# A two-block kernel on one core: first input projection in three fp32r products, first inverse level by transposes, GpSimd's powers ahead of the bias masks

## The chip, the cores and the metric

The kernel runs on one core of a Trainium2 chip. The core has a matrix engine (TensorE, PE in the rows, its weight loads PEld), a vector engine (VectorE, DVE), a scalar engine (ScalarE, ACT), a general engine (GpSimd, POOL) and a queue engine that mostly starts transfers (SyncE, SP). Each runs its own instructions strictly in order and waits on semaphores for the others. The metric is the device time of one launch in microseconds, the median of some runs. One further execution is recorded by the profiler.

## The reference, cut to what matters

Two transformer blocks follow each other on 256 tokens of width 1024. What the change touches is in the first block, and one wait in the second:

```python
h = rmsnorm(x, attn_norm[l])
proj = jnp.einsum('bsd,de->bse', h, w_in[l])          # 1024 -> 3592 columns, fp32
mq, mk, mv, gqkv, gz, ga, gb = jnp.split(proj, offsets, axis=-1)
y_a = moba_attention(...)                             # causal attention on mq, mk, mv
gqkv = jax.nn.silu(causal_depthwise_conv(gqkv, conv_w[l]))
...                                                   # q and k l2-normed, decays from ga, beta from gb
sol = lax.linalg.triangular_solve(eye + A, rhs, left_side=True, lower=True, unit_diagonal=True)
...
x = x + jnp.einsum('bse,ed->bsd', mix, w_out[l])      # then a mixture of experts, then block 2
```

The second block begins with a norm, an input projection, and a norm of the query and key heads (each needs an inverse square root), and its second attention adds a bias with a mask to the scores.

## The kernel before

**Layout and staging.** Everything is fp32. Tokens lie in two blocks of 128. Weights come from memory as units of 1 MB (`unit512`, list `pre`) into a ring of eight slots (`NS = 8`). SP issues unit n+8 when TensorE has used unit n (`freed`). Work is handed over through PSUM banks: three that VectorE empties (`v_bank`, `v_take`), three that ScalarE empties (`a_bank`, `a_take`), each handed out in strict rotation. A bank is asked for only when the third before it has been emptied.

**First projection.** `hT` is the normed input, turned. `cols_T` (L508) computes two pairs of 128 output columns from two units, 256 tokens wide, with the weights as the stationary operand; `rows_nat` (L518) computes 512 output columns with the tokens stationary. A product in fp32 is two instructions in the trace. The order on TensorE is: the three groups of convolution inputs, the 8 gate columns, sums of squares of q and k (L574), the attention's v rows, its q columns, decay rows (L582, L587), its k columns, and z: block 0 ahead of the Gram products (L599 to L614), block 1 behind them.

**Beside it.** ScalarE empties the convolution inputs (`conv_inputs`, L1274), applies silu (L1279) and squares (L1283), then the square roots (L1300), the softplus parts (L1304 to L1307, each with a load of its function table), the attention inputs (L1287), the exponentials of the decays (L1320 to L1323) and z (L1328). VectorE runs three convolutions of four chunks each (`conv`, L1584 and L1586), `qk_norm1` twice (a reciprocal L1616 and a product L1617), and the decay matrices (L1661).

**Inverse.** `X` and `Y` begin as the identity (GpSimd, L2155). At each of seven levels GpSimd masks `BT` (L2162), TensorE multiplies it by `X` (`level_w`, L628), VectorE makes `Wm` of it (L1682), and TensorE multiplies `Y` and `Wm` (L639, L644). Between them stand one head of attention (L655, L662 to L664, L675) and one tile of modulation products (L536, L546).

**The mixture of experts** then streams its weights, and the second block follows. There VectorE's `qk_norm` runs six times: squares and sums, a request to GpSimd for the power -1/2 (`rsqrt` and `power`, L2139), then the products. GpSimd's program has the two bias masks (L2171), which wait for rows that come through a DMA from `rpb_pad`, ahead of these powers. TensorE turns the heads (L929), VectorE copies them (L1969), and the scores begin (L975).

**The split form** is used in the last stage of the program only (`split_product`, L434 to L436; `hidden`, L1077 and L1078): ScalarE rounds a unit to fp32r (the upper part, L1485), VectorE subtracts (the lower part, L2069), and three products upper-upper, lower-upper and upper-lower stand for one in fp32.

## Time and profile before

| | us |
|---|---|
| median of 3 runs | 919.78 |
| lowest and highest | 917.84, 921.96 |
| profiled execution, device time | 921.78 |
| its span, first to last instruction | 920.0 |
| TensorE busy | 838.2 (91%) |
| VectorE busy | 379.5 (41%) |
| ScalarE busy | 258.4 (28%) |
| GpSimd busy | 50.8 (6%) |

The profile's page shows shares of the span. A share is an average over stages that have different limits, so each stage is read in the timeline and in tables of short stretches. The device time of the profiled execution is 1.78 us more than its span, and 2.0 us more than the median.

### The profile page before, as it was taken

The page shows a single profiled execution, that of the slowest core. Times are in us where ns is not written, and L with a number is a line of the kernel's source. Part 1 is how long each engine was busy: PE and PEld are TensorE (multiplying, and loading weights), DVE is VectorE, ACT ScalarE, POOL GpSimd, SP SyncE. Part 2 cuts the span into 40 slices and gives each one's busy share as a digit, 9 for nine tenths or more (in the row PEclk, how much of TensorE's full clock was granted, in tenths as well). Part 3 has the DMA queues.
Part 4 walks back from the last instruction along what each step waited for, and adds up shares of the span by engine and source line. Part 5 has one row for each costly group of instructions (what it writes and reads, how often), then busy time and mean ns, then how long its engine had stood idle before and what let it go on. Part 6 is the DMA issues. An engine that isn't in the chain of part 4 may idle for free.

```text
span 920.0 us, 12562 instructions
## 1 busy us (share of the span) xinstructions
PE 838.2 (91%) x5119; PEld 566.7 (62%) x5119; DVE 379.5 (41%) x710; ACT 258.4 (28%) x416; POOL 50.8 (6%) x35
## 2 busy tenths in 40 slices
PE   8999999989998877677767799979999999999998
PEld 6867767856565432343234254467884788888886
DVE  1557144445260111011101325762424775665765
ACT  2252124421112221122112211034552343443431
POOL 1000042101000000000000004210000000000000
PEclk9999999989999997998899899999999999999999
DMA  9953445557496999999999993420000734654501
GB/s 328 310 193 107 168 183 185 206 205 274 143 385 243 386 408 409 409 409 409 409 408 409 406 317 100 181 92 1 1 1 1 274 137 139 234 176 159 207 1 46
DMA packets 117850, 208.40 MB, mean 227 GB/s; under 512 B 7561, under 2 KB 34474, under 8 KB 117682
## 3 DMA queue, kind: packets, MB, share of 16 engines
q1 hardware_dynamic: 114930, 203.52, 59.9%
q10 hardware_dynamic: 2816, 4.27, 1.6%
q8 instruction: 29, 0.48, 0.2%
q14 instruction: 11, 0.09, 0.0%
q0 software_dynamic: 64, 0.05, 0.0%
HBM read 206.74 MB, written 1.08 MB: 226 GB/s over the span
## 4 chain that ended last, share of the span: by engine, by line
PE 71%; DMA 13%; DVE 7%; issue 3%; POOL 2%; ACT 2%; SPq 2%; DVEq 0%; PEldq 0%; ACTq 0%; POOLq 0%
DMA arena<-in_w_down_dram 10%; PE psa L508 8%; PE psv L1077 5%; PE psa L1077 4%; PE psv L863 4%; PE psa L975 3%; PE psa L847 3%; PE psx L1000 3%; PE psx L536 3%; DMA arena<-rpb_pad 3%; PE psa L798 2%; PE psa L744 2%; PE psv L1078 2%; PE psa L1078 2%; PE psv L518 2%
## 5 line engine op out<-in xcount | busy, mean ns | idle before, releaser
L2069 DVE TENSOR_TENSOR unit_parts<-ring,unit_parts 128x2048 fp32r<-128x2048 f32 x33 | 75.6, 2290 | 59.2 <-ACT unit_parts L1485 59.2
L1485 ACT ACTIVATE unit_parts<-ring 128x2048 fp32r<-128x2048 f32 x33 | 63.2, 1914 | 74.9 <-PE psa L1078 43.8
L905 PE MATMUL psa<-ring,arena 128*128 128x512 f32 (+1 forms) x192 | 76.1, 558 | 2.0 <-DVE arena L1550 1.2
L863 PE MATMUL psv<-ring,arena 128*32 128x256 f32 x1024 | 59.4, 381 | 17.6 <-DMA ring<-in_w_up_dram 13.3
L508 PE MATMUL psa<-arena,ring 128*128 128x256 f32 x320 | 69.9, 380 | 1.0 <-ACT arena L1253 1.0
L1077 PE MATMUL psv<-column_parts,unit_parts 128*128 128x512 f32 (+1 forms) x192 | 67.0, 397 | 2.5 <-DVE arena L2096 1.4
L508 PEld LDWEIGHTS psa<-arena,ring 128*128 128x128 f32 x320 | 60.7, 190 | 10.2 <-DVE arena L1548 1.2
L1077 PE MATMUL psa<-column_parts,unit_parts 128*128 128x512 f32 (+1 forms) x192 | 65.4, 389 | 0.0
L905 PEld LDWEIGHTS psa<-ring,arena 128*128 128x128 f32 x192 | 36.4, 190 | 41.1 <-issue 37.3
L863 PEld LDWEIGHTS psv<-ring,arena 128*32 128x32 f32 x1024 | 32.2, 110 | 42.8 <-DMA ring<-in_w_up_dram 19.1
L1078 PE MATMUL psv<-column_parts,unit_parts 128*128 128x256 f32 (+1 forms) x192 | 52.8, 275 | 0.0
L1078 PE MATMUL psa<-column_parts,unit_parts 128*128 128x256 f32 (+1 forms) x192 | 52.1, 271 | 0.0
L1877 DVE TENSOR_TENSOR arena<-arena,psv 128x256 f32<-128x256 f32 x8 | 3.4, 421 | 116.0 <-ACT arena L1408 116.0
L2139 POOL TENSOR_TENSOR small<-small,consts 128x2 f32<-128x2 f32 (+4 forms) x15 | 21.8, 1454 | 511.5 <-DVE small L1897 274.3
L847 PE MATMUL psa<-arena 128*128 128x128 f32 x256 | 32.3, 287 | 15.5 <-DVE arena L1875 15.5
L847 PEld LDWEIGHTS psa<-arena 128*128 128x128 f32 x256 | 30.8, 201 | 22.1 <-issue 22.1
L1077 PEld LDWEIGHTS psv<-column_parts,unit_parts 128*128 128x128 f32 x192 | 37.1, 193 | 10.3 <-DVE unit_parts L2069 2.8
L1886 DVE TENSOR_TENSOR residual<-residual,psx 128x512 f32<-128x512 f32 x16 | 11.0, 688 | 76.8 <-PE psx L890 76.8
L1077 PEld LDWEIGHTS psa<-column_parts,unit_parts 128*128 128x128 f32 x192 | 36.2, 189 | 7.5
L1078 PEld LDWEIGHTS psv<-column_parts,unit_parts 128*128 128x128 f32 x192 | 37.4, 195 | 0.6 <-issue 0.2
L1078 PEld LDWEIGHTS psa<-column_parts,unit_parts 128*128 128x128 f32 x192 | 36.5, 190 | 0.0
L880 PE MATMUL psx<-arena 128*32 128x512 f32 x128 | 25.6, 896 | 9.6 <-DMA arena<-in_w_down_dram 9.6
(369 smaller groups left out, 1383.4 us busy)
## 6 DMA issues: line engine op xcount, KB each, us to landing
ring<-in_w_gate_dram SPq DMA_DIRECT2D x43, 1024.0 KB, 9.2
ring<-in_w_up_dram SPq DMA_DIRECT2D x43, 1024.0 KB, 5.2
arena<-in_w_down_dram SPq DMA_DIRECT2D x32, 1024.0 KB
ring<-in_w_in_dram SPq DMA_DIRECT2D x28, 1024.0 KB, 9.7
ring<-in_w_mod_dram SPq DMA_DIRECT2D x24, 1024.0 KB, 7.0
ring<-in_w_down_dram SPq DMA_DIRECT2D x11, 1024.0 KB, 7.3
ring<-in_w_out_dram SPq DMA_DIRECT2D x8, 1024.0 KB, 6.0
arena<-rpb_pad ACTq DMA_DIRECT2D x4, 512.0 KB, 16.4
```

Source lines behind the costliest of these rows:

```text
L508: mm = pe.matmul(bank[:, cc * T:(cc + 1) * T], w, hT[:, k, :], start=(k == 0), stop=(k == KD - 1))
L536: mm = pe.matmul(bank[32 * j:32 * j + 32, :], csil[:, k, :], units[r][:, j, :], start=(r == 0), stop=(r == 1))
L847: mm = pe.matmul(mXT[half][:, kk * P:(kk + 1) * P], h2[:, b, k * P:(k + 1) * P], Pd[:, b, :, :].rearrange("p e s -> p (e s)"), start=(b == ...
L863: mm = pe.matmul(mG[32 * e:32 * e + 32, f0:f0 + FF], XT[:, 2 * pair + kk, 32 * e:32 * e + 32], w[:, e, kk * FF:(kk + 1) * FF], start=(pair ...
L880: mm = pe.matmul(mY[half][32 * e:32 * e + 32, :], hidT[:, fc * P + 32 * e:fc * P + 32 * e + 32], w[:, e, :], start=(fc == 0), stop=(fc == 1))
L905: mm = pe.matmul(bank[:, 0:ncols], lhs[:, k, b * P:(b + 1) * P], units[k // per][:, k % per, :], start=(k == 0), stop=(k == KD - 1))
L975: mm = pe.matmul(o_, l_, r_, start=first, stop=last)
L1000: mm = pe.matmul(bank[:, h * HD:(h + 1) * HD], PT2[:, n % 4, m * P:(m + 1) * P], vs[m], start=(m == 0), stop=(m == 3))
L1077: pe.matmul(both_parts(bank, t_0, t_1), hi, col_parts[:, :, k, t_0:t_1], start=(k == 0), stop=False)
L1078: mm = pe.matmul(bank[:, t_0:t_1], lo, col_parts[:, 0, k, t_0:t_1], start=False, stop=(k == KD - 1))
L1485: act.activation(unit_parts[q % 3][:, 0, :], slot_of(NPRE + u_), ACT.Copy).then_inc(upper_done, 1)
L2069: vec.tensor_tensor(lo, slot_of(NPRE + at["mlp"] + 3 * n + kind), hi, ALU.subtract).then_inc(lower_done, 1)
```

## The change

1. **Split projection.** After the first four 128-column groups and the gate columns, which stay in fp32, twelve units (`FIRST_SPLIT` = 3 onward) are used as an upper and a lower part. ScalarE writes the upper part of unit s into one of three buffers (`first_upper_part`), VectorE writes the lower part over the ring slot (`first_lower_part`). The buffers lie over `hn`, `hT` and `mixT`, so upper part s waits until TensorE has used unit s-3 (`freed`). `hT` is split as well, into `row_hi` and `row_lo`; `row_lo` lies over the residual, so x is loaded again later. Eight of the twelve units are now 256 columns wide, with rows of 1 KB in memory instead of 2 KB.
2. **Order.** z is computed whole ahead of the Gram products, and takes both of its banks at the start; the first modulation tile stands behind them. The gate columns and the softplus come earlier on both ScalarE and VectorE.
3. **Level 0 of the inverse** needs no product: `X` and `Y` are not set to the identity any more, the masked `BT` is turned, VectorE writes its `Wm` straight into `X`, and `Y` is the transpose of that.
4. **GpSimd** runs the six `qk_norm` powers ahead of the two bias masks, and TensorE waits for a mask only when the first tile that uses it comes.

```diff
+        FIRST_SPLIT = len(pre)
+        for c0 in (2048, 2304, 2560, 2816):
+            unit512(pre, w_in, c0, 256)
+        unit512(pre, w_in, 1024)
+        for c0 in (0, 256, 512, 768):
+            unit512(pre, w_in, c0, 256)
+        unit512(pre, w_in, 3072)
...
+            def split_cols():
+                hi, lo = split_unit()
+                bank = a_bank()
+                for cc in range(2):
+                    for k in range(KD):
+                        mm = split_product(bank[:, cc * T:(cc + 1) * T], [w[:, k, cc * P:(cc + 1) * P] for w in (hi, lo)],
+                                           [r[:, k, :] for r in (row_hi, row_lo)], k == 0, k == KD - 1)
+                mm.then_inc(a_ready, 1)
+                freed.append((a_ready, na))
...
+            def split_rows(take, ready):
+                banks = [take(), take()]
+                for part in range(2):
+                    hi, lo = split_unit()
...
             def level_w(n):
                 pe.wait_ge(level_masked, n + 1)
-                if n == 0:
-                    pe.wait_ge(inverse_started, 2)
-                else:
+                if n > 0:
                     pe.wait_ge(a_free, na)
...
+                        if n == 0:
+                            mm = pe.transpose(bank[:, h * P:(h + 1) * P], masked, ident)
...
+            def first_upper_part(s):
+                u_ = FIRST_SPLIT + s
+                act.wait_ge(unit_landed[u_ % NS], 16 * (u_ // NS + 1))
+                if s >= 2:
+                    act.wait_ge(*freed[u_ - 3])
+                if s == 2:
+                    act.wait_ge(row_split, 1)
+                act.activation(first_upper[s % 3][:], slot_of(u_), ACT.Copy).then_inc(first_upper_done, 1)
...
+            def first_lower_part(s):
+                dve.wait_ge(first_upper_done, s + 1)
+                u_ = FIRST_SPLIT + s
+                vec.tensor_tensor(ring_parts[:, u_ % NS, :], slot_of(u_), first_upper[s % 3][:],
+                                  ALU.subtract).then_inc(first_lower_done, 1)
...
+            for nh in (2, 2, 8, 8, 8, 8):
+                power(rsn[:, 0:2 * nh])
             pool.wait_ge(s_bias_rows, 64)
```

**ScalarE's order in the first stage.** Before, from the second emptied bank of convolution inputs to the square roots (L1274 convolution inputs, L1279 silu, L1283 squares, L1300 square roots):

```order
L1274 ACTIVATE arena<-psa 128x2x256 [waits a_ready,pad_done]
L1274 ACTIVATE arena<-psa 128x2x256 [waits a_ready] x3
L1279 ACTIVATE arena<-arena 128x1024 [waits conv_done]
L1283 ACTIVATE arena<-arena 128x1024 [waits silu_done]
L1274 ACTIVATE arena<-psa 128x2x256 [waits a_ready]
```

After, the same stretch begins with upper parts 0 and 1 (L1348) and has the convolution inputs (L1356), silu (L1361) and squares (L1365) between them:

```order
L1348 ACTIVATE first_upper<-ring 128x2048 [waits unit_landed3]
L1348 ACTIVATE first_upper<-ring 128x2048 [waits unit_landed4]
L1356 ACTIVATE arena<-psa 128x2x256 [waits a_ready,pad_done]
L1356 ACTIVATE arena<-psa 128x2x256 [waits a_ready]
L1377 ACT_TABLE_LOAD [waits v_free,csil_ready]
L1377 ACTIVATE arena<-vec_cols 128x8 [waits s_const]
L1378 ACTIVATE arena<-vec_cols 128x8
L1348 ACTIVATE first_upper<-ring 128x2048 [waits row_split,v_ready,unit_landed5]
L1361 ACTIVATE arena<-arena 128x1024 [waits conv_done]
L1365 ACTIVATE arena<-arena 128x1024 [waits silu_done]
```

The first two convolution inputs now stand behind the landing of unit 4, and upper part 3 behind the silu of the first convolution.

**ScalarE at the decays** (L1320 and L1418 exponential of the sums, L1323 and L1421 of the decay matrices, L1287 and L1369 attention inputs). Before:

```order
L1287 ACTIVATE arena<-psa 128x512 [waits a_ready] x2
L1320 ACT_TABLE_LOAD
L1320 ACTIVATE small<-small 128x8 [waits log_decay_done]
L1322 ACTIVATE small<-small 128x4 [waits decay_arg_done]
L1323 ACTIVATE arena<-arena 128x1024
L1287 ACTIVATE arena<-psa 128x512 [waits a_ready] x2
```

After:

```order
L1348 ACTIVATE first_upper<-ring 128x2048 [waits a_ready,unit_landed5]
L1418 ACT_TABLE_LOAD
L1418 ACTIVATE small<-small 128x8 [waits log_decay_done]
L1420 ACTIVATE small<-small 128x4 [waits decay_arg_done]
L1421 ACTIVATE arena<-arena 128x1024
L1369 ACTIVATE arena<-psa 128x512 [waits a_ready]
L1348 ACTIVATE first_upper<-ring 128x2048 [waits a_ready,unit_landed6]
```

The last upper part moved behind these exponentials, and so did, as before, the emptying of the third and fourth bank of attention inputs.

**GpSimd in the second half of its program** (L2139 and L2263 are powers, L2171 and L2293 the bias masks). Before:

```order
L2139 TENSOR_TENSOR small<-small,consts 128x8
L2139 TENSOR_TENSOR small<-small,consts 128x2 x2
L2139 TENSOR_TENSOR small<-small,consts 128x4
L2171 TENSOR_TENSOR arena<-arena,consts 128x2048 x2
L2139 TENSOR_TENSOR small<-small,consts 128x4 x2
L2139 TENSOR_TENSOR small<-small,consts 128x16 x4
```

After:

```order
L2263 TENSOR_TENSOR small<-small,consts 128x8
L2263 TENSOR_TENSOR small<-small,consts 128x2 x2
L2263 TENSOR_TENSOR small<-small,consts 128x4 x3
L2263 TENSOR_TENSOR small<-small,consts 128x16 x4
L2293 TENSOR_TENSOR arena<-arena,consts 128x2048 x2
```

Both masks now start directly behind the last of the six powers.

## Rows read from the trace of the kernel before

**Rows 1.** Stretch 60 to 125 us: busy time by engine, granted clock, DMA share, GB/s.

```profile
60.00:125.00 65.00, 65.00 (x259) 44.32 (x258) 32.45 (x51) 18.25 (x25) 6.67 (x4) 1.00 0.35 126
```

**Rows 2.** First 124 us grouped by line: shapes, count, busy us, mean ns, idle before.

```profile
L508 PE MATMUL psa<-arena,ring 128*128 128x256 f32 x320 | 69.9, 380 | 1.0 <-ACT arena L1253 1.0
...
L518 PE MATMUL psv<-ring,arena 128*128 128x512 f32 x32 | 13.9, 592 | 0.0
```

**Rows 3.** Timeline of TensorE's split products: start, duration, line, operands.

```profile
731.94 0.33 PE L1077 MATMUL psa<-column_parts,unit_parts 128*128 128x256 f32 x1
...
732.17 0.33 PE L1077 MATMUL psa<-column_parts,unit_parts 128*128 128x256 f32 x1
...
786.29 0.28 PE L1078 MATMUL psa<-column_parts,unit_parts 128*128 128x256 f32 x1
786.40 0.40 PE L1077 MATMUL psa<-column_parts,unit_parts 128*128 128x512 f32 x1
...
790.25 0.39 PE L434 MATMUL psv<-unit_parts,hidden_parts 128*128 128x512 f32 x1
790.47 0.39 PE L435 MATMUL psv<-unit_parts,hidden_parts 128*128 128x512 f32 x1
```

**Rows 4.** Page, costliest groups: the lower and the upper parts of the last stage.

```profile
L2069 DVE TENSOR_TENSOR unit_parts<-ring,unit_parts 128x2048 fp32r<-128x2048 f32 x33 | 75.6, 2290 | 59.2 <-ACT unit_parts L1485 59.2
L1485 ACT ACTIVATE unit_parts<-ring 128x2048 fp32r<-128x2048 f32 x33 | 63.2, 1914 | 74.9 <-PE psa L1078 43.8
```

**Rows 5.** SP's queue at the fifth unit, and the stretch 31 to 33 us.

```profile
23.79 5.00 SPq L1145 DMA_DIRECT2D ring<-in_w_in_dram  x1
...
31.00:33.00 2.00, 2.00 (x12) 1.75 (x11) 1.86 (x5) 0.00 (x0) 0.00 (x0) 1.00 1.06 402
```

**Rows 6.** Timeline of VectorE and ScalarE: one convolution, a reciprocal, the softplus parts.

```profile
41.60 0.35 DVE L1584 TENSOR_SCALAR arena<-arena,vec_cols 128x256 f32<-128x256 f32 x1 [3.65 <-ACT arena L1274]
...
47.84 1.52 DVE L1586 SCALAR_TENSOR_TENSOR arena<-arena,vec_cols 128x256 f32<-128x256 f32 x3
...
62.49 1.28 ACT L1304 ACT_TABLE_LOAD   x1
...
66.98 6.54 DVE L1616 RECIPROCAL arena<-arena 128x1024 f32<-128x1024 f32 x1
...
68.42 0.20 ACT L1307 ACTIVATE small<-per_head 128x4 f32<-128x4 f32 x1
```

**Rows 7.** Stretches behind a wait of 2.30 us at 198.98: the clock is last but two.

```profile
200.00:203.00 3.00, 2.79 (x12) 2.46 (x13) 0.15 (x1) 0.38 (x1) 0.00 (x0) 0.50 0.12 11
203.00:206.00 3.00, 3.00 (x16) 1.06 (x19) 0.69 (x1) 0.00 (x0) 0.00 (x0) 0.50 0.92 317
```

**Rows 8.** Timeline: TensorE at the first inverse level and at the second.

```profile
123.90 1.95 PE L628 MATMUL psv<-arena 128*128 128x128 f32 x16
...
133.30 2.03 PE L628 MATMUL psv<-arena 128*128 128x128 f32 x16
```

**Rows 9.** Timeline of VectorE and GpSimd around the bias masks and the last power.

```profile
547.24 0.17 DVE L1532 TENSOR_SCALAR small<-small 128x4 f32<-128x4 f32 x1
558.38 0.29 DVE L1937 TENSOR_TENSOR arena<-arena,small 128x128 f32<-128x128 f32 x1 [10.97 <-POOL small L2139]
...
549.79 7.58 POOL L2171 TENSOR_TENSOR arena<-arena,consts 128x2048 f32<-128x2048 f32 x2 [21.88 <-DMA arena<-rpb_pad]
...
598.91 2.90 POOL L2139 TENSOR_TENSOR small<-small,consts 128x16 f32<-128x16 f32 x1 [6.08 <-DVE small L1532]
```

**Rows 10.** Timeline: the last head copies begin on VectorE, the first scores on TensorE.

```profile
604.84 2.12 DVE L1969 COPY arena<-psv 128x256 f32<-128x256 f32 x4
...
611.36 0.71 PE L975 MATMUL psa<-arena 64*128 64x128 f32 x8 [1.12 <-DVE arena L1969]
```

**Rows 11.** Timeline: a product on VectorE and a power on GpSimd that overlap.

```profile
221.52 1.22 DVE L1750 TENSOR_TENSOR arena<-arena 128x1024 f32<-128x1024 f32 x1
...
221.69 2.59 POOL L2139 TENSOR_TENSOR small<-small,consts 128x8 f32<-128x8 f32 x1 [53.08 <-DVE small L1746]
```

More of the change, by code:

```diff
@@ L163, in two_blocks @@
                 end = first + int(np.prod(shape[1:]))
+        first, end = {}, 0
+        with ExitStack() as place:
+            for name, at_, shape in (("first_upper0", 0, [P, SLOT]), ("row_hi", 2048, [P, KD, T]),
+                                     ("first_upper2", 20004, [P, SLOT]), ("first_upper1", 22308, [P, SLOT])):
+                if at_ > end:
+                    place.enter_context(nc.sbuf_tensor(f"before_{name}", [P, at_ - end], F32))
+                first[name] = place.enter_context(nc.sbuf_tensor(name, shape, F32R))
+                end = at_ + int(np.prod(shape[1:]))
+        row_hi = first["row_hi"]
+        first_upper = [first[f"first_upper{n}"] for n in range(3)]
         hid_parts, col_parts = parts["hidden_parts"], parts["column_parts"]
@@ L511, in cols_T, with rows_nat @@
                 freed.extend([(a_ready, na)] * 2)
-            def rows_nat(units, take, ready, ncols=512, blocks=range(NB)):
-                for b in blocks:
+            def rows_nat(units, take, ready, ncols=512):
+                for b in range(NB):
                     bank = take()
@@ L635, in level_xy @@
                 for b in range(NB):
+                    if n == 0:
+                        bank = a_bank()
+                        for h in range(GH):
+                            mm = pe.transpose(bank[:, h * P:(h + 1) * P], X[:, b, h, :], ident)
+                        mm.then_inc(a_ready, 1)
+                        continue
                     if n < LEVELS - 1:
@@ L955, in scores2 @@
                     b, kind, h = tiles2[n]
+                    if kind == 1 and h == 0:
+                        pe.wait_ge(bias_done, b + 1)
                     bank = SB[n % 4]
@@ L2171, in _ @@
                 pl.tensor_tensor(bias[b], bias[b], mask, ALU.add).then_inc(bias_done, 1)
-            for nh in (2, 2, 8, 8, 8, 8):
-                power(rsn[:, 0:2 * nh])
             for b in range(NB):
```

163 lines of the change are left out of this document (110 added, 53 removed).

## The prediction

> **What bounds the kernel now.** I read the table of stretches first. Between 60 and 125 us TensorE is busy for 65.00 of 65 us at the full clock, while VectorE has 32.45 and ScalarE 18.25 us of work [rows 1]. In the stage that is changed, TensorE alone sets the pace and both others have room. The groups by line say what it does: 320 instructions of L508 and two times 32 of L518, all fp32 [rows 2]. The second place is the start of the second block's attention. Its scores begin at 611.36, right behind the last head copy of VectorE [rows 10], and VectorE's chain up to there was held for 10.97 us by a power that stood behind GpSimd's bias masks [rows 9]. Between the two places, the inverse levels run on TensorE without a gap, and what follows hangs on them through weight slots that TensorE frees. So a shift at the start of level 1, 133.30 us [rows 8], should reach the end of the kernel in full.
>
> **Split products on TensorE.** L518's 32 instructions in 13.9 us are 16 products 512 wide at 0.869 us. L508's 320 are 160 products 256 wide at 69.9 / 160 = 0.437 us [rows 2]. In the last stage a split product 512 wide starts 0.22 us behind the other (790.25, 790.47; over a longer row of them 0.2275), so three are 0.68 us. A 256-wide one is followed by the next after 0.11 us (786.29, 786.40), and a pair 256 + 128 wide with two weight loads repeats after 0.23 us (731.94, 732.17) [rows 3]. I take 0.115, which makes 0.345 us for three; the lower bound is half of the 512-wide time, 0.34, and the upper the 0.125 us that are left when 0.2275 is taken from the 0.355 us of a 512 + 256 pair, 0.38. Eight units with 16 products of 256 columns each save 8 x 16 x (0.437 - 0.345) = 11.8 us, four units with 8 products of 512 columns each save 4 x 8 x (0.869 - 0.683) = 6.0 us. That is 17.8 us of TensorE work.
>
> The weight loads are the risk here. The pair of 0.23 us holds two of them, so a load adds at most 0.115 us when it overlaps the work before it [rows 3]. The Trainium skill, "TensorE: Matmul & The Clock Gate", section "LDWEIGHTS (loading the stationary operand)", gives a load of 128 columns about 107 ns. Were that added to each product instead of hidden, three products of 256 columns would take about 0.64 us, more than fp32; the trace of the 256 + 128 pair speaks against it.
>
> **What it adds beside TensorE.** Each unit needs 1.91 us of ScalarE and then 2.29 us of VectorE [rows 4], and the input needs one of each. That is 13 x 2.29 = 29.8 us for VectorE and 24.9 us for ScalarE between 12 and 105 us. The sum fits in the room, so the question is the order. I laid the three programs against each other with the durations of the rows: a convolution 7.8 us (41.60 to 49.36), a reciprocal of 6.54 us with its product of 1.22 us [rows 11], 6.13 us for the four softplus functions with their table loads (62.49 to 68.62) [rows 6]. Four things come out.
>
> *First*, unit 4. SP's issue of it is held for 5.00 us until 28.79, and only at 31 us is the queue at 402 GB/s [rows 5]; the small loads ahead of it take until then. Before, nobody needed this unit before 40. Now upper part 1 waits for it, and the first two convolution inputs wait behind that on ScalarE. One 1 MB unit fewer lies ahead of it, which is worth some 2 us, so I place the landing at 31 us. Then upper part 1 ends at 32.9, lower part 1 at 35.3, the first convolution runs from 35.7 to 43.5, lower part 2 ends at 45.8. TensorE is done with split unit 1 at 41.4: it waits 4.4 us.
>
> *Second*, the sums of squares. The second convolution waits for two more banks of inputs, one of them behind the 6.1 us of softplus on ScalarE (to 54.2), so it ends at 62.6; silu, squares and the emptied bank come at 65.2. TensorE has been ready for the third sum since 58.6: 6.7 us. The fourth wants a bank that comes only after upper part 6, a table load and a square root: 3.0 us more.
>
> *Third*, z. It takes both banks at the start, and its second one is emptied only behind the decay exponentials. These wait for the second `qk_norm1`, which VectorE reaches behind ten lower parts and ends at 105.9. The bank is free at 110.5, TensorE is there at 105.8: 4.8 us.
>
> *Fourth*, level 0. 24 products of 128 columns (48 instructions) become 16 transposes of 0.11 us, some 3.6 us less. But z's second block no longer covers the mask (0.6 us of wait behind the modulation tile), the transposes are shorter than VectorE's 2.1 us for `Wm` (1.2 us), and head 0 of the attention is not ready when they end (2.5 us). This part comes out at nothing.
>
> Together: 17.8 + 3.6 us of work gone, and 0.5 + 4.4 + 6.7 + 3.0 + 4.8 + 0.6 + 1.2 + 2.5 = 23.7 us of waits, with some hand-over. In the laid-out programs level 1 begins at 136.4 instead of 133.3: **+3.1 us**. Each microsecond by which unit 4 lands earlier or later moves it by one (29.5 to 33 us: +1.6 to +5.1).
>
> **The clock.** Behind a wait of 2.30 us at 198.98 TensorE ran at a clock of 0.50 from before 200 to after 206 us, the lower of its levels, 1.2 GHz [rows 7]; elsewhere in this trace the slow stretch was 3.4 us. The first stage had no such wait. Now it has four places with one. A slow stretch of 3.4 us costs 1.7 us where TensorE sets the pace, one of 6.8 us costs 3.4. Behind unit 2 it is swallowed by the next wait. Behind the sums, z and level 0 it is not: 5.1 to 10.2 us. I take 5.5, near the lower end, since part of each stretch can fall into the wait itself. Zero stays as the bound below, since the rows don't say that every wait does it.
>
> **GpSimd's order.** The first power would come at 548.5 instead of 558.4. VectorE's chain then catches up with the projection (its inputs come at 560.4, 574.2 and 587.9), and ends at 599.9 instead of 604.8. TensorE's projection ends at 600.8, so the copies start at 601.3, take the same 6.5 us, and the scores begin at 607.8: -3.6 us. Now the masks, 3.79 us each (7.58 for two) [rows 9], start directly behind the last power, just when VectorE has four products with both inputs in SBUF to do. What such an overlap does is in one place of the trace: a power of 128x8 took 2.59 us on GpSimd, though 128x16 takes 2.90 and 128x4 1.01, which puts 128x8 at 1.64; the 0.95 us more is about the time that VectorE's product of that kind still ran (221.69 to 222.74) [rows 11]. One waits for the other whole. The Trainium skill, "SBUF — State Buffer", section "Who interferes with whom", says so: a VectorE instruction with two SBUF inputs and a GpSimd instruction that reads SBUF share a port under an exclusive lock, and who comes first holds it; the row agrees. Here it speaks against the change, with GpSimd first: one mask ahead of VectorE's products makes this place -3.6 turn into 599.9 + 3.8 = 603.7 against 604.8, **-1.1 us**; both masks make it 607.5, +2.7 us. I take one mask.
>
> The reload of x is 1 MB, at 402 GB/s [rows 5] 2.6 us of a queue that is at 0.35 there [rows 1], and is needed 100 us later: nothing.
>
> **Sum.** 3.1 + 5.5 - 1.1 = +7.5 us on the profiled execution's 921.78 (span 920.0 and 1.78 around it), that is 929.3. Against the median, which lies 2.0 us lower, it is 927.3; I say 927. The bounds: 1.6 + 0 - 3.6 = -2.0 gives 918, 5.1 + 10.2 + 2.7 = +18 gives 938.
>
> **Rivals.**
> *The waits come but are cheap* (27%): the clock falls only once or twice in places that wait anyway, and the masks slip in beside the copies. 3.1 + 1 - 3.6 = +0.5, about 920. For it: each of my waits has an error of 1 to 2 us. Against it: [rows 7] and [rows 11].
> *The parts are in time* (14%): unit 4 lands at 20 us and TensorE stays full. Laid out again with 20 us, level 1 begins 5.1 us earlier, with the tail 8.7 us: 911. If no wait at all were left it would be 17.8 + 3.6 = 21.4 us: 898. For it: the shares of VectorE and ScalarE leave room. Against it: the 5.00 us issue of unit 4 [rows 5], and that VectorE's own chain is long even then. It decides at about 8 us of waits fewer than I count.
> *Both masks and long slow stretches* (8%): 3.1 + 10.2 + 2.7, about 935.
> *Weight loads bind* (3%): at 0.19 us for each 256-wide product (the load's own duration in the profile), 8 x 16 x (0.57 - 0.345) = 28.8 us more work, part of it in the waits: about 945.
> My forecast has 48%.
>
> **How the numbers follow.** About 0.5% (4.6 us) is what a measurement of this kernel can tell from no change. Faster than 915.2 is only the second rival: 15%. Within it are the first rival and the low end of my own case: 25%. Slower: 60%. The range of 8 in 10 runs from 914, which leaves out most of the second rival, to 938.
>
> **What would show it.** In the changed kernel: TensorE idle before its third split unit, before the third sum, and before z, with VectorE and ScalarE named as releasers, and a clock under 1.00 in 45 to 55, 66 to 77 and 112 to 122 us; level 1 (the second group of products by masked `BT`) at 136 to 143 us; starts of 256-wide split products 0.115 us apart; the first of the six powers right behind its request, the masks at about 597, a wait of VectorE there, and scores 1 to 4 us earlier relative to the end of the projection. I am wrong if split unit 2 finds its lower part ready (the chain from unit 4 is then shorter than laid out), or if ScalarE's table loads fall into waits more than I placed them.

## The result, and the profile after

| | us |
|---|---|
| changed kernel, median of 4 runs | 933.53 (929.70 to 935.77) |
| ratio to the kernel before | 1.014, 95% interval 1.0114 to 1.0166 |
| changed kernel again, beside other runs of before | 934.84; ratio 1.0168 (1.0145 to 1.0192) |
| profiled execution: span after, before | 931.8, 920.0 |

The change costs 1.4 to 1.7%. The sign was forecast, the size was not: +7.5 us on record, 13 to 16 measured. For the profiled execution the forecast was 929.3, and it took 933.59. For the median the forecast took off 2.0 us, because the profiled execution of the kernel before was that much slower than its median; the one of the changed kernel lies at its median, so those 2 us came on top of the miss. In the profiled executions the spans differ by 11.8 us, and four places hold all of it.

**The first stage: +9.3 us.** Before, the wait of 2.30 us for the last head of the first attention ended at 198.98 [rows 7]. After, the same wait, TensorE's timeline:

```profile
208.30 0.33 PE L730 MATMUL psv<-consts,arena 128*128 128x128 f32 x1 [2.30 <-DVE arena L1826]
```

TensorE's waits up to 150 us, added up by line and releaser (us in total, times, longest). Before, there was none between 12.6 and 196.7 us:

```profile
PE psa L633 <- ACT arena L1356: 6.1, 1, 6.1
PE psa L453 <- ACT arena L1369: 3.5, 1, 3.5
PE psa L453 <- DVE ring_parts L1682: 3.5, 1, 3.5
PE psv L730 <- DVE arena L1826: 1.8, 1, 1.8
PE psa L633 <- ACT arena L1399: 1.8, 1, 1.8
...
PE psa L701 <- DVE arena L1804: 1.0, 1, 1.0
...
PE psv L689 <- POOL arena L2282: 0.6, 1, 0.6
```

In the forecast's order these are: split unit 2 (the 3.5 of L1682), the third and the fourth sum (6.1 and 1.8), z (the 3.5 of L1369), and in level 0 the mask, `Wm` and head 0 (0.6, 1.0, 1.8). The timeline of ScalarE and VectorE shows the chain behind the first of them, link for link as laid out:

```profile
32.32 1.91 ACT L1348 ACTIVATE first_upper<-ring 128x2048 fp32r<-128x2048 f32 x1 [13.90 <-DMA ring<-in_w_in_dram]
34.13 1.06 ACT L1356 ACTIVATE arena<-psa 128x512 f32<-128x512 f32 x2
...
36.87 0.35 DVE L1696 TENSOR_SCALAR arena<-arena,vec_cols 128x256 f32<-128x256 f32 x1
...
44.56 2.29 DVE L1682 TENSOR_TENSOR ring_parts<-ring,first_upper 128x2048 fp32r<-128x2048 f32 x1
```

Upper part 1 waits 13.90 us for unit 4, the two convolution inputs come behind it, the first convolution (L1696) begins at 36.87, and lower part 2 ends at 46.85, where TensorE goes on (46.90).

Stretches of the changed kernel (columns as in [rows 1]; the granted clock is last but two; 0.50 is the lower level, 1.2 GHz):

```profile
31.50:35.00 3.50, 3.50 (x20) 3.50 (x18) 0.74 (x1) 2.68 (x3) 0.00 (x0) 0.51 1.09 387
...
65.50:69.00 3.50, 2.04 (x2) 0.50 (x2) 3.43 (x5) 3.48 (x4) 0.00 (x0) 0.52 0.00 0
69.00:75.50 6.50, 5.34 (x11) 3.56 (x12) 6.04 (x14) 2.85 (x5) 0.00 (x0) 0.50 0.01 3
113.50:117.00 3.50, 3.39 (x8) 2.72 (x9) 1.66 (x1) 3.48 (x4) 0.00 (x0) 0.52 0.32 121
140.50:144.50 4.00, 4.00 (x22) 3.95 (x21) 1.73 (x6) 0.00 (x0) 0.00 (x0) 0.57 0.62 240
525.50:529.50 4.00, 4.00 (x11) 1.18 (x4) 0.40 (x1) 0.60 (x1) 0.00 (x0) 0.50 1.06 395
```

At half the clock, half of TensorE's busy time in a slow stretch is lost: 1.7, 1.0, 2.7, 1.6 and 1.7 us in the first stage, **8.7 us** together. Three of these places lie behind a wait, as forecast. The one at 31.5 us has no wait ahead of it.

Not all of the 8.7 us is paid. The slow stretch at 31.5 us ends ahead of the wait for split unit 2, and another engine sets the end of that wait. In a second run with the same first stage ("masks first", below) the stretch lasted 6.8 us instead of 3.4, and the wait was shorter and ended at the same time (in the four other profiles with this order it ends between 45.9 and 46.7, after 0.8 to 2.9 us). The first row is of the changed kernel, the second of that run:

```profile
46.90 0.39 PE L453 MATMUL psa<-row_hi,first_upper 128*128 128x256 f32 x1 [3.45 <-DVE ring_parts L1682]
46.91 0.38 PE L453 MATMUL psa<-row_hi,first_upper 128*128 128x256 f32 x1 [1.82 <-DVE ring_parts L1682]
```

The same holds for the 1.0 us at the third sum: the fourth begins 3.80 us behind the third here, where the third runs slowly (66.36 and 70.16 us), and in "convolution first", below, where it runs at the full clock (58.22 and 62.02). So 1.7 and 1.0 us only shorten the next wait, and **6.0 us** of the clock are paid.

**The bias masks: +2.4 us.** The scores begin 12.9 us behind the end of the projection (611.87 to 624.76); before it was 10.5 (600.84 to 611.36 [rows 10]). GpSimd's and VectorE's timelines after:

```profile
604.97 2.90 POOL L2263 TENSOR_TENSOR small<-small,consts 128x16 f32<-128x16 f32 x1 [6.08 <-DVE small L1631]
607.84 7.59 POOL L2293 TENSOR_TENSOR arena<-arena,consts 128x2048 f32<-128x2048 f32 x2
...
607.90 3.77 DVE L1635 TENSOR_SCALAR small<-small 128x16 f32<-128x16 f32 x1 [3.01 <-POOL small L2263]
611.71 4.26 DVE L2061 TENSOR_TENSOR arena<-arena,small 128x512 f32<-128x512 f32 x1
616.00 0.69 DVE L2063 TENSOR_TENSOR arena<-arena,qk_gains 128x512 f32<-128x512 f32 x1
...
618.07 1.34 DVE L2093 COPY arena<-psv 128x256 f32<-128x256 f32 x3
```

L1635, the rescaling behind the last power, takes 0.17 us elsewhere in this trace and the product L2061 0.69. Here each lasts nearly one whole mask (3.79 us) longer: 3.6 and 3.6 us. TensorE waits 5.63 us for the copies, until 618.54, and its clock falls there too.

**The mixture of experts: +1.7 us**, a slow stretch at its end (the last row above) longer than the one before the change, and **the last stage: -1.6 us**, a slow stretch at 728.5 us of the kernel before that this execution did not have. Both are the clock of one execution: nothing was changed in the mixture of experts, and from the last head of the first attention to the end of block 2's projection the 16 profiles of this document take 398.1 to 403.6 us, this one the most, the kernel before 401.9. Sum: 9.3 + 2.4 + 1.7 - 1.6 = 11.8.

### The profile page after: what moved, and what is told of

It reads as the page before. It is cut to its first block, busy times and chain, and to the rows that moved or that the text cites. A ratio compares the mean times of both kernels' runs of the same rounds, so it can differ in the third digit from the quotient of the medians.

```text
span 931.8 us, 12861 instructions
## 1 busy us (share of the span) xinstructions
PE 835.5 (90%) x5247; PEld 573.2 (62%) x5247; DVE 415.6 (45%) x723; ACT 281.7 (30%) x428; POOL 48.8 (5%) x33
## 4 chain that ended last, share of the span: by engine, by line
PE 65%; DMA 11%; DVE 11%; SPq 4%; issue 4%; ACT 3%; POOL 1%; DVEq 0%; PEldq 0%; POOLq 0%; ACTq 0%
DMA arena<-in_w_down_dram 10%; PE psa L974 5%; PE psv L1146 4%; PE psa L1146 4%; PE psa L1044 3%; PE psa L916 3%; PE psx L1069 3%; PE psv L932 3%; PE psx L595 2%; PE psa L867 2%; PE psa L813 2%; PE psv L1147 2%; PE psa L1147 2%; PE psx L959 2%; PE psv L1053 2%
## 5 line engine op out<-in xcount | busy, mean ns | idle before, releaser
L932 PEld LDWEIGHTS psv<-ring,arena 128*32 128x32 f32 x1024 | 32.7, 110 | 36.2 <-DMA ring<-in_w_up_dram 11.8
L2263 POOL TENSOR_TENSOR small<-small,consts 128x2 f32<-128x2 f32 (+4 forms) x15 | 21.8, 1454 | 537.3 <-DVE small L2021 275.9
L916 PE MATMUL psa<-arena 128*128 128x128 f32 x256 | 32.3, 287 | 15.5 <-DVE arena L1999 15.5
L1146 PEld LDWEIGHTS psv<-column_parts,unit_parts 128*128 128x128 f32 x192 | 36.1, 188 | 10.4 <-DVE unit_parts L2193 2.8
L1146 PEld LDWEIGHTS psa<-column_parts,unit_parts 128*128 128x128 f32 x192 | 36.1, 188 | 7.5
L453 PE MATMUL psa<-row_hi,first_upper 128*128 128x256 f32 x128 | 37.4, 292 | 3.5 <-DVE ring_parts L1682 3.5
L1682 DVE TENSOR_TENSOR ring_parts<-ring,first_upper 128x2048 fp32r<-128x2048 f32 x12 | 27.3, 2287 | 24.1 <-ACT first_upper L1348 24.1
L454 PE MATMUL psa<-row_hi,ring_parts 128*128 128x256 f32 x128 | 36.7, 287 | 0.0
L1147 PEld LDWEIGHTS psv<-column_parts,unit_parts 128*128 128x128 f32 x192 | 36.3, 189 | 0.6 <-issue 0.2
L455 PE MATMUL psa<-row_lo,first_upper 128*128 128x256 f32 x128 | 36.7, 286 | 0.0
```

The source lines that it names most:

```text
L453: pe.matmul(o, l[0], r[0], start=first, stop=False)
L454: pe.matmul(o, l[1], r[0], start=False, stop=False)
L455: return pe.matmul(o, l[0], r[1], start=False, stop=last)
L916: mm = pe.matmul(mXT[half][:, kk * P:(kk + 1) * P], h2[:, b, k * P:(k + 1) * P], Pd[:, b, :, :].rearrange("p e s -> p (e s)"), start=(b == ...
L932: mm = pe.matmul(mG[32 * e:32 * e + 32, f0:f0 + FF], XT[:, 2 * pair + kk, 32 * e:32 * e + 32], w[:, e, kk * FF:(kk + 1) * FF], start=(pair ...
L1146: pe.matmul(both_parts(bank, t_0, t_1), hi, col_parts[:, :, k, t_0:t_1], start=(k == 0), stop=False)
```

## The experiments

All ratios are to the kernel before, run beside them. "Turn to scores" is the time from the end of the projection of block 2 (the first turned head) to the first score: 10.5 us before, 12.9 after.

### The masks

**Masks first** puts the masks back ahead of the six powers.

```diff
+            pool.wait_ge(s_bias_rows, 64)
+            for b in range(NB): ...        # the two masks
             for nh in (2, 2, 8, 8, 8, 8):
                 power(rsn[:, 0:2 * nh])
-            pool.wait_ge(s_bias_rows, 64)
-            for b in range(NB): ...
```

> The changed kernel, with the two bias masks of GpSimd put back ahead of the six qk_norm powers; everything else as changed. My theory: with the masks behind the last power, VectorE's last rescaling and its next product each stood behind one whole mask (3.77 and 4.26 us instead of 0.17 and 0.69), so the head copies began 10.2 us behind the last power instead of 3.0. With the masks first, VectorE's chain is the one of the kernel before, held for 11 us by the first power: copies 3.8 us behind the end of the projection instead of 6.1, scores about 2.3 us earlier, and the whole about 931.2 against 933.5. Rival (the later scores come from the slower clock behind the wait, not from the masks): no change.

Measured: 928.36 us, ratio 1.0087 (1.0054 to 1.012), 5 us off the changed kernel. Turn to scores 9.1 us. That is 3.8 less than after, and 1.4 less than before, probably since the projection now runs later against VectorE's chain.

**Masks late** leaves them behind the powers and adds one wait.

```diff
             for nh in (2, 2, 8, 8, 8, 8):
                 power(rsn[:, 0:2 * nh])
+            pool.wait_ge(qk2_normed, 6)
             pool.wait_ge(s_bias_rows, 64)
```

> The changed kernel, with one more wait on GpSimd: the two bias masks start only when VectorE has ended the last of its qk_norm products. My theory: the masks block only VectorE's instructions on SBUF; its last chain is then undisturbed and ends about 1 us before the projection does, the copies begin right behind the projection, and the scores begin 6.5 us behind it instead of 12.8: 5.5 to 6.3 us off, about 928. If the head copies (from PSUM to SBUF) are blocked by a mask as well, each mask holds one of them: the gain is then 0 to 2 us.

Measured: 925.70 us, ratio 1.0062 (1.0039 to 1.0084), 7.8 us off. Turn to scores 6.0 us. GpSimd and VectorE of this run:

```profile
609.99 7.60 POOL L2294 TENSOR_TENSOR arena<-arena,consts 128x2048 f32<-128x2048 f32 x2 [3.19 <-DVE arena L2063]
...
606.83 0.17 DVE L1635 TENSOR_SCALAR small<-small 128x16 f32<-128x16 f32 x1 [3.01 <-POOL small L2263]
607.04 0.69 DVE L2061 TENSOR_TENSOR arena<-arena,small 128x512 f32<-128x512 f32 x1
...
611.23 5.53 DVE L2093 COPY arena<-psv 128x256 f32<-128x256 f32 x10 [1.31 <-PE psv L998]
```

The rescaling and the product are back at 0.17 and 0.69 us. The ten copies from PSUM run through both masks without being held (0.55 us each; before, four took 2.12 [rows 10]). So it is the lock. It held the two instructions that work on SBUF alone, and none of the copies from PSUM.

**The same two on the kernel before**: only the fourth part of the change, and then the fourth part with the late masks.

```diff
             power(both_rstd)
-            pool.wait_ge(s_bias_rows, 64)
-            for b in range(NB): ...
             for nh in (2, 2, 8, 8, 8, 8):
                 power(rsn[:, 0:2 * nh])
+            pool.wait_ge(qk2_normed, 6)       # in the second of the two only
+            pool.wait_ge(s_bias_rows, 64)
+            for b in range(NB): ...
...                                        # TensorE waits for a mask at the first tile that uses it
```

> The kernel before, with only the fourth part of the change: the six powers ahead of the two bias masks, and a wait of TensorE for a mask at the first tile that uses it. My theory (both masks block VectorE, one whole mask each): the scores begin 12.9 us behind the end of the projection instead of 10.6, as in the changed kernel: 922 against 920. The prediction on record had one mask of 3.8 us in the way and 1.1 us of gain: 919.

> The kernel before, with the powers ahead of the masks and the masks behind VectorE's last qk_norm product. As in the changed kernel with late masks, the scores begin 6.0 us behind the end of the projection instead of 10.6, and the slow stretch of TensorE that fell into that wait may go: 915 to 916 against 920. Rival (the first part of VectorE's chain, which waits 11 us less now, is only moved into waits for the projection): above 918.

Measured: powers first 923.89, ratio **1.0052 (1.0034 to 1.007)**; masks late 916.85, ratio **0.9973 (0.996 to 0.9987)**. The fourth part of the change by itself is a loss of 4.9 us, and one more wait makes it a gain of 2.1. The change alone, VectorE:

```profile
598.56 3.77 DVE L1537 TENSOR_SCALAR small<-small 128x16 f32<-128x16 f32 x1 [3.01 <-POOL small L2140]
602.37 4.26 DVE L1938 TENSOR_TENSOR arena<-arena,small 128x512 f32<-128x512 f32 x1
```

The same two holds to the hundredth. The turn-to-scores times are 13.6 and 6.0 us, so the traces have 3.0 us of loss and 4.5 of gain at this place. The medians have 4.9 and 2.1. In both profiles the last head of the first attention comes 1.7 and 1.6 us later than before (200.68 and 200.59 against 198.98), behind one slow stretch of 3.4 us that begins at 58.7 and 59.0 (below). With it the scores come 4.7 us later and 3.2 earlier, nearer to the medians. The first stage's program is the same in all three kernels, so why the other executions should have this stretch as well is not shown.

### The order of the split projection

**Convolution first** moves one upper part on ScalarE and one lower part on VectorE.

```diff
             first_upper_part(0)
-            first_upper_part(1)
             ...
             conv_inputs(0)
             conv_inputs(1)
+            first_upper_part(1)
...
             first_lower_part(0)
-            first_lower_part(1)
             ...
             conv(0)
+            first_lower_part(1)
             first_lower_part(2)
```

> The changed kernel, with upper part 1 on ScalarE moved behind the first two convolution inputs, and lower part 1 on VectorE behind the first convolution, so that neither stands behind the landing of unit 4. My theory: the waits before split unit 2 (3.45 us), before the third and fourth sums (6.07 and 1.76 us) and half of that before z all come from VectorE starting its first convolution at 36.9 instead of 27.5 us. They go, a wait of up to 2 us before split unit 1 comes, and the slow stretch of TensorE from 65.7 to 75.7 us goes too: 10 to 15 us off, 919 to 924. Rival (VectorE's own sum of work bounds the stage, so that waits only move to z): no more than 4 us off.

Measured: 925.64, ratio 1.0068 (1.0048 to 1.0087), 7.9 us off, less than the 10 expected. The first convolution begins at 27.30 instead of 36.87. TensorE's waits up to 125 us:

```profile
PE psa L453 <- ACT arena L1368: 3.5, 1, 3.5
PE psa L633 <- ACT arena L1399: 2.7, 1, 2.7
PE psa L633 <- ACT arena L1355: 1.6, 1, 1.6
```

The wait ahead of split unit 2 is gone and 6.1 has become 1.6, but the one ahead of the fourth sum stayed (2.7 instead of 1.8, because the third sum ran at the full clock here; both fourth sums begin 3.80 us behind the third), and z kept its 3.5. The miss tells something: these two waits don't come from the late start. What is left to move is the softplus with its table loads, which stands between two convolutions, and the decay exponentials ahead of z's bank.

**Split order** moves these as well.

```diff
-            (softplus: Exp, Ln, Sigmoid, Exp)      # ScalarE, ahead of conv_inputs(3)
...
             for n in range(4): ...                 # the square roots
+            first_upper_part(6)
+            (softplus)
...
             first_upper_part(10)
+            moba_inputs(2)
+            first_upper_part(11)
+            moba_inputs(3)
             (exponentials of the decays)
-            moba_inputs(2)
-            first_upper_part(11)
-            moba_inputs(3)
...                                        # the softplus result moves on VectorE too
```

> The order of the run before (upper and lower part 1 behind the first convolution), and two more changes of order. The softplus on ScalarE, with its four table loads, and its result on VectorE come behind the square roots; upper part 6 behind them too. The third and fourth bank of attention inputs and upper part 11 come ahead of the exponentials of the decays. No instruction is added or taken away. My theory: the waits of TensorE in the split projection are this order and nothing else. The 1.6 and 2.7 us around the sums shrink to under 1 us, the 3.5 us before z go, and with them their slow stretches (1.7 and 3.3 us): 10 to 12 us off the run before, 913 to 916, faster than the kernel before. Rival (VectorE's sum of work is the bound of the stage): 922 or more.

Measured: **914.73, ratio 0.9943 (0.9922 to 0.9964)**, faster than the kernel before, 10.9 us off the last run. The waits of TensorE up to 114 us:

```profile
PE psv L647 <- DVE arena L1753: 2.8, 1, 2.8
...
PE psa L633 <- ACT arena L1393: 0.2, 1, 0.2
```

No instruction was taken out of the program. The trace has one load of a function table fewer on ScalarE (11 instead of 12 up to 200 us, 1.28 us each), which came with the order. The waits of the split projection were order, but for what that one load is worth. What is left, 2.8 us ahead of the decay rows' sums, is the only one of the rival's kind: VectorE reaches a copy late behind a reciprocal of 6.55 us.

### Level 0

> The changed kernel with level 0 of the inverse as before: X and Y set to the identity by GpSimd, 16 products for W and 8 for Y instead of 16 transposes, X and Y both emptied by ScalarE. The rest as changed, the modulation tile ahead of level 0 too. My theory: the transposes save 3.6 us of TensorE work and give it back in waits (0.56, 0.97, 1.82 us) and in the slow stretch from 140.7 to 144.4 us that follows them (1.7 us). With the products there is work where those waits are; I expect level 1 within 1 us of where it is, and the slow stretch gone: 0 to 2 us off, 931.5 to 933.5. Rival (the transposes are worth their 3.6 us): 937.

> The changed kernel with one change of order: the scores of head 0 on TensorE, and their maximum on VectorE, come ahead of the modulation tile and of level 0, not between its transposes. My theory: head 0 is then ready when the second group of transposes ends, and the mask is ready when the first begins; the waits of 0.56 and 1.82 us go, that on Wm stays or grows by 0.9 us: level 1 begins some 1.5 to 2.5 us earlier, and if no wait over 1 us is left the slow stretch behind it goes as well (1.7 us). 929.5 to 932. Rival (VectorE, which does the maximum and Wm one after the other, keeps the waits as they are): no change.

The first undoes the third part of the change, the second only moves head 0:

```diff
-            mod_products(MOD_LEVELS[0])
...
+                if n == 0:
+                    moba_scores(0)
+                    mod_products(MOD_LEVELS[0])
                 if n < LEVELS:
                     level_w(n)
```

Measured: 929.89 (ratio 1.012, 1.009 to 1.0149) and 929.28 (1.0111, 1.0083 to 1.0139). Both are 4 us off, and neither should be credited with it: in the traces the last head of the first attention comes within 1 us of where it was, and the rest is won in the mixture of experts (398.8 and 398.3 us to the end of the projection, against 403.6), which neither edit touches. TensorE with level 0 in products, from its first product to that of level 2:

```profile
133.66 2.05 PE L690 MATMUL psv<-arena 128*128 128x128 f32 x16 [0.49 <-POOL arena L2279]
...
142.30 2.03 PE L690 MATMUL psv<-arena 128*128 128x128 f32 x16
...
152.58 2.03 PE L690 MATMUL psv<-arena 128*128 128x128 f32 x16
```

and in the changed kernel, with transposes:

```profile
133.97 1.09 PE L689 MATMUL psv<-consts,arena 128*128 128x128 f32 x8 [0.56 <-POOL arena L2282]
...
141.22 3.42 PE L691 MATMUL psv<-arena 128*128 128x128 f32 x16
...
152.89 2.03 PE L691 MATMUL psv<-arena 128*128 128x128 f32 x16
```

Level 1 comes after 8.64 us with products and 7.25 with transposes, level 2 after **18.92 us in both**. The 1.39 us that the transposes win are lost in the slow stretch at 140.5, which the products, with no wait over 0.51 us there, don't have. In this pair of profiles the transposes are worth nothing, as forecast, and the clock takes 1.4 us of it. In the other six profiles with transposes in this place and order, the slow stretch is longer, and the last head comes 75.3 to 77.5 us behind the first transpose, where these two have 74.3: there the transposes lose 0.9 to 3.2 us against this one profile with products. With head 0 first, two waits of 1.82 and 0.76 us are left, the slow stretch comes all the same, and level 1 follows level 0 after 7.02 us instead of 7.25. That expectation, 1.5 to 2.5 us, was too high.

### The clock

**Filled waits** puts products that nobody reads into three waits.

```diff
+                    keep_busy(4)          # ahead of split unit 2
...
+                    keep_busy(8 or 2)     # ahead of the third and fourth sum
...
+            keep_busy(5)                  # ahead of z
```

> The changed kernel, with products on TensorE that nobody reads, put into three of its waits: 4 ahead of split unit 2, 8 and 2 ahead of the third and fourth sums, 5 ahead of z (0.67 us each, less than the wait in each place). My theory: it is the waits that let the clock fall, so the slow stretches from 65.7 to 75.7 and 113.5 to 116.9 us go, which cost 4.1 and 1.6 us: about 928. Rival (the split products themselves bring the clock down, as at 31.5 us, where no wait stands ahead): the slow stretches stay or move, and the time stays within 1.5 us of 933.5.

Measured: 927.82, ratio 1.0088 (1.0057 to 1.012), 5.7 us off, as expected. In the trace the last head of the first attention comes 3.9 us sooner, and the rows show the clock there:

```profile
65.00:69.00 4.00, 3.38 (x6) 1.04 (x6) 3.89 (x6) 3.97 (x4) 0.00 (x0) 0.57 0.00 0
69.00:76.00 7.00, 6.82 (x29) 5.05 (x28) 6.57 (x14) 2.12 (x4) 0.00 (x0) 1.00 0.01 2
112.00:118.00 6.00, 6.00 (x28) 4.84 (x27) 2.23 (x1) 1.68 (x2) 0.00 (x0) 1.00 0.13 19
```

The stretch at z is at full clock, that at the sums is cut from 10.2 us to 3.4 (2.5 us of wait were left there), and the two places without filling are slow still, at 31.3 for 3.4 us and at 133.7 for 6.8. Where the wait ahead of z is not filled, 3.5 us long, all seven profiles that have it show a slow stretch there. So a wait can let the clock fall, and the work behind the wait pays. Not every wait does: behind the 3.45 us ahead of split unit 2 the clock stayed at 1.00 in the first profile of the changed kernel, and fell at 47.6 us in the second.

**The stretch at 31 us** has no wait ahead. Two runs, both built on the run with all orders (below), looked for its cause:

```diff
-            for _ in range(4):
-                split_cols()
+            (split unit 0 as fp32 products from hT)
+            for _ in range(3):
+                split_cols()
```

> The run with all changes of order, and the first of the twelve split units computed in fp32 again (7.0 us instead of 5.7 on TensorE; one upper and one lower part fewer). This is for the slow stretch that begins at 30.0 to 31.5 us in every run with a split projection and has no wait ahead of it. If the begin of the split products brings it, it moves with them, to 38 us or later; if something else does at that time, it stays at 31. By work alone the kernel is 1.3 us slower (909.5), less what VectorE and ScalarE gain: 908 to 910.

```diff
                 for k in range(KD):
+                    pe.matmul(PSX[1][:, 0:T], row_hi[:, k, 0:P], row_hi[:, k, :], start=True, stop=True)
                     mm = pe.matmul(bank[:, 0:8], hT[:, k, b * P:(b + 1) * P], gate[:, k, :],
                                    start=(k == 0), stop=(k == KD - 1))
```

> The run with all changes of order, and one fp32r product of 128x256 that nobody reads ahead of each of the 16 products of the gate columns, which are 8 columns wide. The slow stretch at 30 to 31.5 us stayed where it was with the first unit in fp32, so the split products don't bring it; it begins behind 3.7 us of these narrow products in each split kernel, and behind them at 58.5 us in two runs built on the kernel before. If narrow products count for the clock like a wait, the stretch at 30 goes: 16 x 0.12 = 1.9 us are added and 1.75 come back, the time stays at 908 to 909, and the clock there is 1.00. If it stays, the gate columns are not its cause, and the kernel takes 910.

(`PSX[1]` is a bank that nobody reads there.) Measured: 909.74 (ratio 0.9904, 0.9881 to 0.9927) and 909.52 (0.9892, 0.9852 to 0.9932). A row of each, in that order:

```profile
31.00:34.80 3.80, 3.80 (x12) 3.03 (x11) 3.51 (x9) 2.98 (x2) 0.00 (x0) 0.55 1.09 386
```

```profile
30.50:37.00 6.50, 6.50 (x32) 6.50 (x32) 6.18 (x11) 4.87 (x5) 0.00 (x0) 0.51 1.09 385
```

The stretch stays with the first unit in fp32, so the split products don't bring it. It stays with wide products between the narrow ones too (6.8 us long, as in four profiles without them), but that doesn't clear the narrow ones, as the gate products of the changed kernel, of the last run and of the kernel before show:

```profile
26.71 3.74 PE L537 MATMUL psv<-ring,arena 128*128 128x8 f32 x32
```

```profile
29.56 0.36 PE L630 MATMUL psx<-row_hi 128*128 128x256 f32 x1
29.76 0.28 PE L631 MATMUL psv<-ring,arena 128*128 128x8 f32 x2
29.90 0.40 PE L630 MATMUL psx<-row_hi 128*128 128x256 f32 x1
```

```profile
54.58 3.63 PE L518 MATMUL psv<-ring,arena 128*128 128x8 f32 x32
```

With the filling, 0.14 of each 0.34 us still belong to the narrow products. In 15 of the 16 profiles the fall begins 2.6 to 4.8 us behind the first of these products, whether they stand at 27 us or, in the two runs built on the kernel before, at 54.5; in six of them, the filled run among them, it begins while they run. Only the kernel before has them without a fall. So the narrow products stay the nearest suspect, and the cause stays open.

### All orders together

> All changes of order together: that of the split projection, head 0 ahead of level 0, and the bias masks behind VectorE's last qk_norm product. If the three places are independent, their gains add: 914.5 - 2 - 7 = about 905, 1.5% faster than the kernel before. If a shorter first stage is given back in the mixture of experts, whose transfers set their own pace, it stays above 912.

> The run with all changes of order, and on VectorE the decay rows, the two copies of the v rows and lower part 8 ahead of the first qk_norm1 (its reciprocal of 6.55 us) instead of behind it. It had one wait left in the split projection, 2.80 us at 81.8 us for the second of these copies, with a slow stretch of 4 us behind it. Both should go: 2.8 + 2.0 = 4.8 us off, 903.5. Rival (VectorE is behind by as much, so that z or the inverse waits instead): 906 to 908.

The first joins the split order, head 0 first and the late masks. The second adds one move on VectorE:

```diff
-            qk_norm1(0)
-            first_lower_part(8)
             (decay rows, copies of the v rows)
+            first_lower_part(8)
+            qk_norm1(0)
```

Measured: **908.18 us, ratio 0.9873 (0.9847 to 0.9899)**: 25 us under the changed kernel and 1.3% under the kernel before, 3 us short of the 905 expected. The wait for the last head of the first attention ends at 190.18 us instead of 198.98, and turn to scores is 6.0. Against the kernel before with late masks (916.85), the split projection with level 0 in transposes is worth 8.7 us once it is ordered. The second run has 908.35 (0.9877, 0.9859 to 0.9894), no gain where 4.8 us were expected. Its waits up to 119 us:

```profile
PE psa L700 <- DVE arena L1807: 1.8, 1, 1.8
PE psa L453 <- DVE ring_parts L1685: 1.8, 1, 1.8
```

The 2.8 us went, and 1.8 us came ahead of z, for a lower part. That fits the rival, VectorE's sum of work, but another order on VectorE was not tried, so it is not shown. A slow stretch of 6.8 us at 119.9 took back the rest.

### The changed kernel again

> The changed kernel itself, once more, beside the three that follow. Each of the runs with one order undone or moved came out 2 to 3 us below what its trace explained. If that is chance between groups of runs, this one measures 930.5 to 932; if the trace readings miss something, it is at 933.5 again.

Measured: 934.84, not 931. So it is not chance between groups of runs: the six single moves gained 0.6 to 5.2 us more in their medians than their traces show at the place that was moved. Against the first profile of the changed kernel the surplus lies in the mixture of experts, from the last head to the end of the projection: 398.3 to 401.5 us with a move, 403.6 without. The second profile has 400.1 there and loses elsewhere. In it the slow stretches of the first stage are longer (one more at 47.6, and 10.2 us instead of 3.4 from 139.8), and the last head of the first attention comes 2.5 us later, at 210.83. Why a move in one stage should change the clock in another is not shown.

## Why the prediction was off

Its sum was 3.1 (work and waits) + 5.5 (clock) - 1.1 (masks) = +7.5.

*Split products*: mis-sized a little, by 2.4 us. Two split units with 256 columns lie between 46.90 and the sums at 58.41, 5.75 us each and 0.120 us for a product, where 0.115 was taken; the products 512 wide follow each other after 0.232 instead of 0.2275. Eight units save 6.99 - 5.75 each, four 6.95 - 5.57: 15.4 us, not 17.8. The weight loads don't bind, which was the risk weighed there. (Two figures beside the sum are a little off: 0.355 - 0.2275 is 0.1275, not 0.125, and 0.345 us plus three loads of 107 ns is 0.67, not 0.64.)

*Waits*: right in every place and releaser, and most of them a little too long: 3.5, 6.1, 1.8, 3.5, 0.6, 1.0 and 1.8 make 18.2 us, where 23.7 were laid out. The 2.7 us that the slow clock took out of two of them belong to them, which makes 20.9, and the error 2.8 us. Unit 4 was in use at 32.3, forecast 31. The rival that the parts are in time was never near in this order, and the order alone decided it: the run with the split order is it.

*Clock*: right in its mechanism, which the filled waits show, and near in size: 6.0 us are paid, behind the sums, z and level 0, the three places that the forecast named, where it took 5.5. The stretch at 31.5 us that no wait precedes was not forecast; here it costs nothing. -15.4 - 3.6 + 20.9 + 6.0 makes 7.9; the trace has 9.3, and 1.4 is left to hand-overs.

*Masks*: this is the step that failed. It read: "I take one mask", -1.1 us. Both masks held VectorE, +2.4 us in the trace; with this part of the change alone, 3.0 us in the trace and 4.9 in the median. I had looked at the four products with two inputs in SBUF and overlooked the `TENSOR_SCALAR` of the last power ahead of them, 0.17 us of work [rows 9]. It met the first mask; GpSimd took the second in the gap behind it, and so the first product met that one. The upper bound of that step, +2.7, was both masks, and the page I cited says enough: the Trainium skill, "SBUF — State Buffer", section "Who interferes with whom", counts `tensor_scalar` among the instructions that can take the shared ports, and whichever engine comes first holds them for its whole instruction. The two holds of 3.6 us agree. That section has `copy` in the same list; the copies of this kernel read PSUM, and they were not held.

*Level 0* came out at nothing in the profile after, as forecast, though by waits and clock, and at a loss in six others.

Term by term: work and waits 3.3 us (9.3 - 6.0) instead of 3.1, clock 6.0 instead of 5.5, masks 2.4 instead of -1.1. That makes 11.7, where 7.5 were forecast and the spans differ by 11.8. The masks are 3.5 of these 4.2 us. That the first term came out within 0.2 us is luck: the split saves 2.4 us less than laid out and the waits are 2.8 us shorter, and 0.6 us more go to hand-overs (1.4 where the forecast had 0.8). The measured time lies inside the range of 914 to 938, whose upper bound had both masks.

## What to carry to other kernels

Before an engine with slack is given work for one that has none, lay its program out instruction by instruction: here the waits stood behind instructions that nobody needed yet, and the same instructions in another order, with one wait more on GpSimd, were 25 us faster. Count a wait of TensorE in such a place at more than its length: here 18.2 us of waits brought 7.0 us of lost clock behind them, of which 6.0 were paid. That ratio is of this kernel alone, and a slow stretch that ends ahead of another wait costs nothing. And a long GpSimd instruction on SBUF must not stand where VectorE has even one short instruction on SBUF in its chain: put it under VectorE's copies from PSUM.

## What the runs showed of the hardware that was not expected

- GpSimd's masks of 3.79 us held VectorE twice in a row, 3.6 us each, because a `TENSOR_SCALAR` of 0.17 us stood between them. Ten copies from PSUM (5.53 us) ran through the same masks unheld.
- TensorE's clock falls to 1.2 GHz for 3.4 to 6.8 us also in places where it is busy and has no wait: at 29.3 to 31.5 us in all 13 profiles with the split projection, and at 58.7 and 59.0 us in the two of the kernel before with the powers first. Ahead of each stand the 32 instructions of the gate columns, 8 columns wide; the first unit in fp32 or in fp32r makes no difference. The kernel before has the same instructions and no fall, so why is open.
- Split products 256 wide with a weight load each follow each other after 0.120 us at the full clock.
- A slow stretch ahead of a wait whose end another engine sets costs nothing: 3.4 or 6.8 us of it at 30 us, and split unit 2 begins at 46.90 and 46.91.
